# RWKV heads: GpSimd masks behind the spread of blocks, four things in other places, two projection steps moved

## The chip, the cores and the metric

One core of a Trainium2 chip. The metric is the device time of one execution of the whole program, in microseconds. A core has five engines with queues of their own that meet only at semaphores: TensorE (PE, matrix products into eight PSUM banks), VectorE (DVE), ScalarE (ACT), GpSimd (POOL) and SyncE (SP, which here only issues DMAs). PEld is TensorE's loading of weights.

## The reference, cut to what matters

The program is a two-layer trunk: in each layer three token mixers side by side (SSD, RWKV-7, neighbourhood attention), a gated merge, and a mixture of experts. Only the RWKV mixer is touched. It computes, for 16 heads of width 64, in two directions, over 256 context and 256 latent tokens:

```
p = p + mu * bi_shift(p);  r, k, v, wl, al, gl = split(p)
w = -softplus(-(w0 + tanh(wl) @ w2)) - 0.5;  decay = exp(-exp(w))
a = sigmoid(a0 + al @ a2);  g = sigmoid(gl) @ g2
kk = normalise(k * k_k);  k_dir = k * (1 + (a - 1) * k_a)
S = S * w_t - (S kk_t) (kk_t * a_t)' + v_t k_t';  y_t = S r_t      # scan, both directions
yn = (y - mean) * rsqrt(var + eps) * ln_w + ln_b
out = (yn + bonus) * g
```

In layer 0 outputs are wanted for all 512 tokens, in layer 1 for the 256 latent ones only.

## The kernel before, in words

`rwkv_heads` (from line 1679) does a layer in eight turns, one for each pair of heads (128 channels on the 128 partitions). The scan is done in chunks of 64 tokens, eight chunks (`NC`), two heads and two directions at a time. Within a chunk the delta rule needs the inverse of a triangular 64x64 matrix. It is made from 16x16 blocks on VectorE (`block_inverses`, lines 2558 to 2581: transposes, small products, and the spread of the blocks into their place, line 2580 and its neighbours), and widened to 64 with products on TensorE in four stages (`STAGES`; TensorE's `inverse(b, g)`). ScalarE and VectorE take each stage's products out of PSUM (`EVACUATIONS`: "copy" is ScalarE's line 2277, "vcopy" VectorE's line 2590, "eye" adds the unit matrix on VectorE, line 2594). Then the inverse is applied (`apply_inverse`; the result leaves PSUM by ScalarE's line 2287 and VectorE's line 2599), the chunk products are made, and `crossing` carries the state over the chunks in six chain steps (TensorE `step`, VectorE `chain`, line 2619).

The order of the work is written out by hand. Each engine has a function `mix(b, c, ...)` for a turn, in which b is the turn whose scan is carried out and c the next one, whose features are prepared beside it. TensorE's `filler(n)` puts n projection steps of turn c (24 in all: three column groups of eight steps, each a product of 128x128 weights with 512 tokens; in layer 1 the last group has 256 tokens) into places at which it would otherwise wait. In the last turn, which has no c, the filler does 40 steps of gate projections of 512 (layer 1: 256) tokens instead, and the tuple `LAST` says how many at each call. An assertion holds that all steps are done.

The places that the change touches:

- GpSimd's `masks` (line 2419) multiplies the gram matrices by triangular masks, four instructions (line 2417). It waits until VectorE has transposed the first of two results of the block inverse (`X_TURNED`, step 28 of 33 of semaphore `small`, line 2575). VectorE's second transpose (2577) and the four instructions of line 2580 follow.
- ScalarE's `root` (line 2294) turns the variance of a finished turn into a reciprocal root: a logarithm (line 2296, from PSUM bank `SUM_BANK` = 0) and an exponential (line 2298). It stands in the next turn's `mix`, behind `key_grams(b, 1)`. TensorE waits for the logarithm (semaphore `vlog`) before `decay_and_rate(0)` writes the same bank (lines 1846, 1847). The variance product is line 2044.
- ScalarE's `gate` copies the gate product out of bank 4 (line 2193). It stands behind `keep_middle(c, 0)` (line 2180) and the load of the logarithm's table (line 2330). TensorE's `gram_times_v` waits for it and for VectorE's `bound_norm` (line 2473), as both banks are written anew.
- VectorE's `mix` (line 2631): `shift_key` (lines 2453, 2455) stands before `inverse(b, 1)`, and `apply_inverse` (line 2599) behind `shift_mix(3)` (2464), `unit_key` (2487) and two `key` (2491). ScalarE's `key_square` (2189) and the second `decay_and_rate` (2184, 2185) wait for the shifted key, and TensorE's gate product (line 1851) for those.
- VectorE's `out` (lines 2625, 2628, 2629) finishes the turn before, and `bonus` (line 2515) takes bank 3 out, for which the third group of products in stage 1 waits.
- GpSimd's other work in a turn: `inner_decays` (2399, 2400), `receptance` (2406), `copy_receptance` (2413).

Of the kernel before, what the change touches and what calls it, by code (L numbers as in the profile page):

```python
# [1678 lines left out]
def rwkv_heads(k, y, t0):  # L1679
# [9 lines left out]
    with ExitStack() as st:  # L1689
# [129 lines left out]
        def _(pe):  # L1819
# [167 lines left out]
            def crossing(b, c, kept, filler):  # L1987
                if b:
                    hold(s.g3in, b(4, 4))
                    hold(s.rin, b(2, 2))  # L1990
                    step(b, 1)
                    filler(2)
                    step(b, 2)
                if c:
                    hold(s.rawin, kept)
                    value_turns(c)
                if b:
                    filler(1)
                    step(b, 3)
                    for pos in range(1, 4):  # L2000
                        for z in range(2):
                            across(z, pos)
                if c:
                    key_turns(c, 0)
                if b:
                    filler(1)
                    step(b, 4)
                    for z in range(2):
                        across(z, 4)
                if c:  # L2010
                    key_turns(c, 1)
                if b:
                    filler(2)
                    step(b, 5)
                    for z in range(2):
                        across(z, 5)
                if c:
                    left_turns(c)
                if b:
                    step(b, 6)  # L2020
                    for z in range(2):
                        across(z, 6)
                if b and not c:
                    filler(2)
                if c:
                    hold(s.rdec, c(2, 2))
                    gram_pair(c, 0, 0, [(s.tok, c(8, 5)), (s.tok, c(8, 6))])
                if b:
                    for z in range(2):
                        hold((s.st0, s.st1)[z], b(6, 6))  # L2030
                        across(z, 7, s.y_done if z else None)
                if c:
                    gram_pair(c, 0, 1, [(s.tok, c(8, 7)), (s.tok, c(8, 8))], s.gdone)
                    gram_other(c)
                    if b:
                        filler(2)
                        variance(b)
                    for part in range(2):
                        gram_pair(c, 1, part, [] if part else [(s.nevac, c(6, 6)), (s.nevac, c(6, 5))], s.gdone)
                    bonus(c)  # L2040
# [2 lines left out]
                pe.wait_ge(s.sq, b(1, 1))  # L2043
                mm(k.bank[SUM_BANK][:, 0:n], const(k, "headones"), yq[:, t0:], start=True, stop=True).then_inc(s.var_d, 1)

            LAST = (7, 7) + 13 * (2,)

            def mix(b, c, raws, ended, gating=False):
                at = [0, 0]

                def late_gates(count):
                    for _ in range(LAST[at[1]]):
                        i, kt = at[0] // KT, at[0] % KT
                        if kt == 0:
                            hold(tile_in[LATE_PLACE[i]], 16 * LATE_LOADS[i])
                            if i < 2:
                                hold(s.rawin, raws)
                            else:
                                hold(s.sig_done, i - 1)
                            if i == 1:  # L2060
                                hold(s.gevac, b(4, 4))
                        gate_step(3 + i, kt, LATE_PLACE[i], LATE_BANKS[i], s.gate_done)
                        at[0] += 1
                    at[1] += 1

                def filler(count):
                    if not c:
                        late_gates(count)
                        return
                    for _ in range(count):  # L2070
                        j, kt = STEP_ORDER[at[0] // KT], at[0] % KT
                        if kt == 0:
                            hold(w_in[j], b(16, 16))
                        if at[0] == 0:
                            hold(s.rawin, raws)
                        if at[0] == KT:
                            hold(s.gevac, b(4, 4))
                        if at[0] == 2 * KT:
                            hold(s.rawin, b(3, 7))
                        if gating:  # L2080
                            gate_step(at[0] // KT, kt, j, RAW_BANK[j], s.proj)
                        else:
                            projection_step(j, kt)
                        at[0] += 1

                filler(4)
                if c:
                    hold(s.low_in, c(32, 32))
                    if ended:
                        hold(s.vlog, ended(1, 1))  # L2090
                    decay_and_rate(0, RATE_BANKS)
                filler(4)
                inverse(b, 0)
                filler(1)
                inverse(b, 1, filler)
                filler(1)
                if c:
                    hold(s.wa_in, c(4, 2))
                    decay_and_rate(1, RATE_BANKS)
                inverse(b, 2)  # L2100
                if c:
                    gate_and_norm(c)
                filler(1)
                if c:
                    hold(s.gate_in, c(1, 1))
                    hold(s.normin, c(1, 1))
                gram_times_v(b)
                inverse(b, 3)
                filler(1)
                apply_inverse(b)  # L2110
                filler(1)
                chunk_products(b, filler)
                inside(b)
                crossing(b, c, b(3, 8), filler)
                assert at[0] == (3 * KT if c else 5 * KT), at

# [50 lines left out]
        def _(act):  # L2167
# [23 lines left out]
            def gate(c, at):  # L2191
                act.wait_ge(s.gate, c(1, 1))
                ac(y[:, at, t0:], one(k.bank[GATE_BANK][:, 0:n]), ACT.Copy).then_inc(s.gate_in, 1)
# [100 lines left out]
            def root(b):  # L2294
                act.wait_ge(s.var_d, b(1, 1))
                ac(yq[:, t0:], k.bank[SUM_BANK][:, 0:n], ACT.Ln, scale=1.0 / 64, bias=fixed[:, 1:2]).then_inc(s.vlog, 1)
                act.wait_ge(s.vlog, b(1, 1))
                ac(yq[:, t0:], yq[:, t0:], ACT.Exp, scale=-0.5).then_inc(s.root, 1)

# [8 lines left out]
            def mix(b, c, at, ended, gating=False):  # L2308
                key_grams(b, 1)
                if ended:  # L2310
                    root(ended)
                if c:
                    act.wait_ge(s.pcd, c(1, 1))
                    keep_middle(c, 1)
# [8 lines left out]
                if c:  # L2323
                    keep_middle(c, 2)
                    key_square(c)
                    decay_and_rate(1, c, RATE_BANKS)
                    key_rates(c)
                    act.wait_ge(s.vb, b(MIX_STEPS, SET_UP + 1))
                    keep_middle(c, 0)
                    nc.scalar.preload_act_table_set("natural_log")  # L2330
                    gate(c, at)
                    inverse_norm(c)
                gram_times_v(b)
                if not c:
# [15 lines left out]
                if c:  # L2350
                    gram(c)
                    keep(STEP_ORDER[2], c, b(3, 9), gating=gating)
                    key_grams(c, 0)
                    off_blocks()
                else:
                    root(b)

            first = turn_value(0)
            act.wait_ge(s.derived, 1)
# [34 lines left out]
        def _(pool):  # L2394
# [22 lines left out]
                tt(ops[:, h, j, chunks], ops[:, h, j, chunks], spread(mask(name, h), chunks.stop - chunks.start), ALU.mult).then_inc(s.masked, 1)  # L2417

            def masks(b):
                pool.wait_ge(s.small, b(BLOCK_STEPS, X_TURNED))  # L2420
                pool.wait_ge(s.gevac, b(4, 4))
                for j, name in ((IN_KEY, "strict"), (OUT_KEY, "inclusive")):
                    for h in range(2):
                        with_mask(b, h, j, name)
# [18 lines left out]
        def _(v):  # L2443
# [187 lines left out]
            def mix(b, c, m, f, i, before, ahead):  # L2631
# [3 lines left out]
                    out(m, *before)  # L2635
                bonus(m, b)
                m.settle()
                if c:
                    v.wait_ge(s.rpd, b(2, 2))
                    v.wait_ge(s.rawin, c(3, 3))  # L2640
                    v.wait_ge(s.pcd, c(1, 1))
                    shift_key(f, c)
                inverse(b, 1)
                if c:
                    sums(f, c, 0)
                inverse(b, 2)
                if c:
# [4 lines left out]
                if c:  # L2652
                    shift_sum(f, c, 2)
                    shift_mix(f, c, 2, 2, vv)
                    shift_sum(f, c, 0)
                    shift_mix(f, c, 3, 0, r)
                    unit_key(f, c)
                    key(f, c, 0)
                    key(f, c, 1)
                apply_inverse(b)  # L2660
                if c:
                    f.settle()
                    away(f, c, 0)
                chunk_moves(b)
# [1104 lines left out]
```

## Time and profile before

| | us |
|---|---|
| median of 3 runs | 3647.39 (3645.66 to 3649.04) |
| the profiled execution | 3645.4 |
| its span | 3643.6 |
| mean granted TensorE clock | 0.966 of full |
| RWKV heads, first seven turns, layer 0 | 482.4 |
| RWKV heads, first seven turns, layer 1 | 448.4 |
| the eighth turns' start | 1391.7 and 3158.4 |

Times in rows are microseconds from the span's start. A row of a timeline gives start, duration, engine, line, operation, and the tiles or tensors it writes and reads; "x4" is a run of four instructions merged into a row. What stands in square brackets is the idle time of that engine just before, and what ended it. In the rows of busy time by stretch the columns are: the stretch, its length, the busy time of PE, PEld, DVE, ACT and POOL with their numbers of instructions, the granted clock of TensorE as a share of full speed, the DMA share and GB/s.

### The profile page before, as it was taken

How to read it: one execution, taken by the hardware profiler on the slowest of the kernel's cores; microseconds unless marked ns; L12 is line 12 of the kernel's file. 1: busy time of each engine (PE TensorE's matmuls, PEld its weight loads, DVE VectorE, ACT ScalarE, POOL GpSimd, SP SyncE). 2: the span in 40 equal slices, each digit the busy share in tenths (PEclk: the TensorE clock that was granted, in tenths of full speed). 3: DMA queues.
4: the chain of work that ended last, by engine and by line, in shares of the span. 5: the costliest groups of instructions: out<-in, count | busy, mean ns of one | idle time of the engine just before them, and what ended most of it. 6: DMA issues, size and time to landing. Idle time of an engine off the chain costs nothing. (4 is left out here: it accounts for less than half of the span.)

```text
span 3643.6 us, 72098 instructions
## 1 busy us (share of the span) xinstructions
PE 3283.6 (90%) x31390; PEld 1789.5 (49%) x31390; DVE 1686.4 (46%) x3268; ACT 1082.8 (30%) x1940; POOL 453.5 (12%) x411
## 2 busy tenths in 40 slices
PE   6989999998888889999999697998988888899997
PEld 3454444544555555443332345656655555674333
DVE  3584902664777774220000356834257777631111
ACT  2211001603655653121111321103145656420001
POOL 0051200401111110010000002112011111100000
PEclk8999999999999999999999799999999999899998
DMA  5103623252111111369998211834211111269996
GB/s 205 52 19 110 202 71 96 81 169 57 28 28 30 28 34 54 111 253 420 407 386 345 91 47 47 265 111 110 78 43 28 36 28 30 55 239 383 424 424 275
DMA packets 255436, 537.18 MB, mean 147 GB/s; under 512 B 49520, under 2 KB 173696, under 8 KB 222224
## 3 DMA queue, kind: packets, MB, share of 16 engines
q1 hardware_dynamic: 236064, 463.82, 34.8%
q0 software_dynamic: 19056, 68.69, 5.4%
q8 instruction: 254, 4.16, 0.5%
q14 instruction: 62, 0.51, 0.0%
HBM read 514.59 MB, written 17.87 MB: 146 GB/s over the span
## 5 line engine op out<-in xcount | busy, mean ns | idle before, releaser
L1295 PE MATMUL banks<-sb_h,sb_ring 128*128 128x512 f32 (+1 forms) x1344 | 474.8, 512 | 11.3 <-DMA sb_ring<-w_branch 7.7
L1295 PEld LDWEIGHTS banks<-sb_h,sb_ring 128*128 128x128 f32 x1344 | 254.3, 190 | 225.0 <-issue 195.8
L1832 PE MATMUL banks<-sb_h,sb_ring 128*128 128x512 f32 (+1 forms) x672 | 325.6, 604 | 6.3 <-DMA sb_ring<-w_in 4.1
L815 PE MATMUL banks<-sb_h,sb_ring 128*128 128x512 f32 x512 | 232.6, 613 | 19.4 <-SPq L237 19.4
L1823 PE MATMUL banks<-inv 64*64 64x64 f32 x4864 | 141.9, 233 | 62.1 <-DVE inv L2594 37.8
L1823 PEld LDWEIGHTS banks<-inv 64*64 64x64 f32 x4864 | 121.6, 145 | 140.5 <-issue 139.3
L3393 DVE TENSOR_TENSOR hrow<-hrow,banks 128x256 f32<-128x256 f32 x36 | 15.1, 421 | 356.2 <-ACT hrow L3429 356.2
L3241 PE MATMUL banks<-gu,xs 128*64 128x512 f32 x768 | 169.3, 594 | 4.1 <-DMA gu<-gu_pairs 3.6
L1832 PEld LDWEIGHTS banks<-sb_h,sb_ring 128*128 128x128 f32 x672 | 119.4, 197 | 108.5 <-issue 92.4
L1295 PE MATMUL banks<-sb_branch,sb_ring 128*128 128x512 f32 (+1 forms) x512 | 170.9, 487 | 0.0
L815 PEld LDWEIGHTS banks<-sb_h,sb_ring 128*128 128x128 f32 x512 | 100.0, 198 | 139.1 <-issue 118.4
L578 DVE SCALAR_TENSOR_TENSOR sc<-vtok,first_silu,sc 128x1024 f32<-128x1024 f32 x112 | 149.3, 1374 | 7.0 <-DMA vtok<-w_mod 1.2
L3521 PE MATMUL banks<-gu,xs 128*32 128x512 f32 x1368 | 150.1, 592 | 2.2 <-ACT xs L3414 2.2
L1295 PEld LDWEIGHTS banks<-sb_branch,sb_ring 128*128 128x128 f32 x512 | 96.9, 190 | 68.7 <-issue 60.6
L1525 DVE TENSOR_TENSOR sb_acc<-zs,banks 128x512 f32<-128x512 f32 (+1 forms) x16 | 8.9, 553 | 251.8 <-PE banks L1295 251.8
L1295 PE MATMUL banks<-sb_ring,sb_h 128*128 128x512 f32 x256 | 110.2, 592 | 0.0
L3241 PEld LDWEIGHTS banks<-gu,xs 128*64 128x64 f32 x768 | 53.8, 137 | 113.8 <-issue 101.1
L3521 PE MATMUL banks<-sb_ring,xs 128*32 128x512 f32 x936 | 103.8, 593 | 1.4 <-ACT xs L3414 0.8
L1837 PE MATMUL banks<-sb_h,sb_ring 128*128 128x512 f32 (+1 forms) x256 | 103.9, 535 | 0.0
L2417 POOL TENSOR_TENSOR ops<-ops,sb_consts 128x512 f32<-128x512 f32 (+1 forms) x64 | 72.9, 1170 | 247.5 <-DVE inv L2575 247.5
L1115 DVE SCALAR_TENSOR_TENSOR W<-W,sb_cols 128x512 f32<-128x512 f32 x128 | 100.7, 787 | 4.5
L3521 PEld LDWEIGHTS banks<-gu,xs 128*32 128x32 f32 x1368 | 48.9, 110 | 98.6 <-issue 95.7
(502 smaller groups left out, 5641.2 us busy)
## 6 DMA issues: line engine op xcount, KB each, us to landing
gu<-gu_pairs SPq DMA_DIRECT2D x64, 1536.0 KB, 16.8
gu<-gu_tiles SPq DMA_DIRECT2D x57, 1024.0 KB, 9.3
sb_ring<-w_in SPq DMA_DIRECT2D x24, 2048.0 KB, 9.3
sb_ring<-gu_tiles SPq DMA_DIRECT2D x39, 1024.0 KB, 9.9
vtok<-w_mod POOLq DMA_DIRECT2D x64, 512.0 KB, 5.6
sb_ring<-down_pairs SPq DMA_DIRECT2D x32, 1024.0 KB, 14.7
sb_ring<-w_in SPq DMA_DIRECT2D x58, 512.0 KB, 3.9
sb_ring<-down_tiles SPq DMA_DIRECT2D x25, 1024.0 KB, 8.5
```

Source lines behind the costliest of these rows:

```text
L578: do.put(nc.vector.scalar_tensor_tensor(self.acc[c], tile, by, self.acc[c], ALU.mult, ALU.add))
L815: m = mm(k.bank[j], k.ring[:, h, kt, P * j:P * j + P], k.h[:, kt], start=kt == 0, stop=kt == KT - 1)
L1115: tap.do(stt(out, src, w, out, ALU.mult, ALU.add))
L1295: mm = nc.tensor.matmul(out, left(kt), right(kt), start=kt == 0, stop=kt == KT - 1)
L1525: tt(k.acc[:, t, t0:], sg[:, t % 2, t0:], projs[0][t % 2][:, 0:n], ALU.mult).then_inc(s.merged, 1)
L1823: m = mm(k.bank[bank][H[to], at:at + w], left, right, start=start, stop=True, skip_group_check=True)
L1832: m = mm(k.bank[banks[j]][:, WHOLE[j]:], w[:, j, kt], k.h[:, kt, WHOLE[j]:], start=kt == 0, stop=kt == KT - 1)
L1837: m = mm(k.bank[bank][:, t0:], parts.tiles[place][:, kt], k.h[:, kt, t0:], start=kt == 0, stop=kt == KT - 1)
L2417: tt(ops[:, h, j, chunks], ops[:, h, j, chunks], spread(mask(name, h), chunks.stop - chunks.start), ALU.mult).then_inc(s.masked, 1)
L3241: m = mm(wide[i][rows[e], :], xs[:, kt, rows[e]], cols[:, 512 * i:512 * i + 512], start=kt == 0, stop=kt == KT - 1)
L3393: nc.vector.tensor_tensor(h, h, wide[i][:, 256:512], ALU.mult).then_inc(s.mul, 1)
L3521: m = mm(banks[i][32 * j:32 * j + 32], left[:, P * i + 32 * j:P * i + 32 * j + 32], w[:, e], start=start, stop=stop)
```

## The change

```diff
 TensorE, crossing:
                 if b:
-                    filler(1)
                     step(b, 3)
...
                 if b:
-                    filler(1)
                     step(b, 4)
...
-            LAST = (7, 7) + 13 * (2,)
+            LAST = (8, 8) + 9 * (2,) + (3, 3)
...
                     decay_and_rate(0, RATE_BANKS)
-                filler(4)
+                filler(6)
                 inverse(b, 0)

 ScalarE:
             def root(b):
                 act.wait_ge(s.var_d, b(1, 1))
                 ac(yq[:, t0:], k.bank[SUM_BANK][:, 0:n], ACT.Ln, scale=1.0 / 64, bias=fixed[:, 1:2]).then_inc(s.vlog, 1)
+
+            def root_end(b):
                 act.wait_ge(s.vlog, b(1, 1))
                 ac(yq[:, t0:], yq[:, t0:], ACT.Exp, scale=-0.5).then_inc(s.root, 1)
...
                 key_grams(b, 1)
                 if ended:
-                    root(ended)
+                    root_end(ended)
...
                     key_rates(c)
+                    gate(c, at)
+                    nc.scalar.preload_act_table_set("natural_log")
                     act.wait_ge(s.vb, b(MIX_STEPS, SET_UP + 1))
                     keep_middle(c, 0)
-                    nc.scalar.preload_act_table_set("natural_log")
-                    gate(c, at)
                     inverse_norm(c)
...
                     keep(STEP_ORDER[2], c, b(3, 9), gating=gating)
+                    root(b)
                     key_grams(c, 0)
                     off_blocks()
                 else:
                     root(b)
+                    root_end(b)

 GpSimd:
             def masks(b):
-                pool.wait_ge(s.small, b(BLOCK_STEPS, X_TURNED))
+                pool.wait_ge(s.small, b(BLOCK_STEPS, BLOCK_STEPS))
                 pool.wait_ge(s.gevac, b(4, 4))

 VectorE, mix:
                 m.settle()
+                inverse(b, 1)
                 if c:
...
                     shift_key(f, c)
-                inverse(b, 1)
-                if c:
                     sums(f, c, 0)
                 inverse(b, 2)
...
                     shift_sum(f, c, 0)
+                apply_inverse(b)
+                if c:
                     shift_mix(f, c, 3, 0, r)
                     unit_key(f, c)
                     key(f, c, 0)
                     key(f, c, 1)
-                apply_inverse(b)
-                if c:
                     f.settle()
                     away(f, c, 0)
                 chunk_moves(b)
```

The work of each engine is the same as before. The logarithm of a turn's variance now stands in that turn's own crossing, before the gram copies of the next; the exponential stays where it was.

## Rows read from the trace of the kernel before

**Rows 1.** The page, busy time of each engine over the whole span.
```profile
PE 3283.6 (90%) x31390; PEld 1789.5 (49%) x31390; DVE 1686.4 (46%) x3268; ACT 1082.8 (30%) x1940; POOL 453.5 (12%) x411
```
**Rows 2.** Busy time by stretch: seven turns of layer 0, seven of layer 1.
```profile
909.32:1391.68 482.36, 417.28 (x9020) 263.79 (x9019) 355.50 (x710) 280.05 (x448) 81.14 (x71) 0.97 0.12 31
2710.04:3158.43 448.39, 369.78 (x8525) 250.97 (x8523) 338.11 (x711) 265.88 (x448) 73.67 (x70) 0.95 0.13 35
```
**Rows 3.** TensorE's waits, layer 0's seven turns: releaser, total us, times, longest.
```profile
PE banks L1823 <- DVE inv L2594: 21.6, 7, 3.4
PE banks L1950 <- DVE inv L2599: 15.2, 7, 2.2
PE banks L1823 <- ACT sb_branch L2193: 9.7, 7, 1.4
PE banks L1823 <- ACT inv L2261: 8.0, 6, 1.3
```
**Rows 4.** The same view, layer 1's seven turns.
```profile
PE banks L1950 <- DVE inv L2599: 18.1, 7, 2.8
PE banks L1823 <- DVE inv L2594: 15.3, 7, 2.5
PE banks L1823 <- ACT sb_branch L2193: 11.7, 7, 2.0
PE banks L1823 <- ACT inv L2261: 11.3, 6, 1.9
```
**Rows 5.** Timeline of a layer 0 turn: masks, and VectorE's spread before and beside them.
```profile
1046.83 5.06 POOL L2417 TENSOR_TENSOR ops<-ops,sb_consts 128x512 f32<-128x512 f32 x4 [15.09 <-DVE inv L2575]
...
1044.19 1.45 DVE L2573 TENSOR_SCALAR inv<-x,sb_consts 64x256 f32<-64x256 f32 x4
...
1048.56 3.76 DVE L2580 TENSOR_SCALAR inv<-inv,sb_consts 64x256 f32<-64x256 f32 x4
```
**Rows 6.** Timeline at 881 us (GpSimd, VectorE), and line 2497 in a turn.
```profile
881.21 3.08 POOL L2406 TENSOR_TENSOR cc<-cc,rkv 128x512 f32<-128x512 f32 x2 [30.77 <-ACT cc L2214]
...
881.41 1.75 DVE L2497 TENSOR_TENSOR sb_ring<-bb 128x512 f32<-128x512 f32 x1
...
1081.63 0.68 DVE L2497 TENSOR_TENSOR sb_ring<-bb 128x512 f32<-128x512 f32 x1
```
**Rows 7.** Timeline of TensorE behind its wait for line 2594.
```profile
1055.17 1.81 PE L1832 MATMUL banks<-sb_h,sb_ring 128*128 128x512 f32 x2
1056.91 2.96 PE L1823 MATMUL banks<-inv 64*64 64x64 f32 x64
1059.80 1.13 PE L1832 MATMUL banks<-sb_h,sb_ring 128*128 128x512 f32 x2
```
**Rows 8.** Timeline, the shifted key and what follows it on ScalarE.
```profile
1057.51 0.75 DVE L2455 SCALAR_TENSOR_TENSOR rkv<-sb_ring,pc,rkv 128x512 f32<-128x512 f32 x1
...
1058.30 0.72 ACT L2189 ACTIVATE sb_ring<-rkv,pc 128x512 f32<-128x512 f32 x1 [0.46 <-DVE rkv L2455]
...
1062.06 0.69 ACT L2184 ACTIVATE sb_ring<-banks,pc 128x512 f32<-128x512 f32 x1 [3.04 <-PE banks L1847]
```
**Rows 9.** Timeline of ScalarE around the gate copy.
```profile
1066.80 0.60 ACT L2193 ACTIVATE sb_branch<-banks 128x512 f32<-128x512 f32 x1
```
**Rows 10.** Timeline of VectorE and GpSimd around the applied inverse and the chunk moves.
```profile
1073.21 0.75 DVE L2464 SCALAR_TENSOR_TENSOR rkv<-sb_ring,pc,rkv 128x512 f32<-128x512 f32 x1
...
1075.98 1.28 DVE L2599 COPY inv<-banks 128x512 f32<-128x512 f32 x2
...
1077.37 2.85 POOL L2406 TENSOR_TENSOR cc<-cc,rkv 128x512 f32<-128x512 f32 x2 [6.70 <-ACT cc L2214]
...
1078.63 0.69 DVE L2605 TENSOR_TENSOR inv<-banks,sb_consts 128x512 f32<-128x512 f32 x1 [0.77 <-PE banks L1950]
```
**Rows 11.** Timeline of ScalarE, the table loads of the root.
```profile
1040.64 1.28 ACT L2296 ACT_TABLE_LOAD   x1
...
1042.64 1.28 ACT L2298 ACT_TABLE_LOAD   x1
```

## Prediction

> **What bounds the kernel now.** I read the page first: TensorE is busy for 90% of the span, every other engine for under half [rows 1]. That is a mean over stages, and the change touches one stage, the RWKV heads. It runs twice (layer 0 from about 909 us, layer 1 from about 2710 us), each time in eight turns. So the second view is the busy time of the first seven turns of each layer: 482.4 us with 417.3 us of TensorE in layer 0, 448.4 us with 369.8 us in layer 1 [rows 2]. TensorE stands idle for 65.1 us and 78.6 us there, 9.3 us and 11.2 us a turn, in turns of 68.9 us and 64.1 us. Its mean granted clock is 0.97 and 0.95 of full; with the two levels 2.4 and 1.2 GHz that is 2 x 0.03 x 482 = 29 us and 2 x 0.05 x 448 = 45 us at the lower one. VectorE is busy for 50.8 us and 48.3 us of a turn and so not far behind. All that can be won is in these 144 us of waits, in at most half of those 74 us of slow clock, and in little beside it.
>
> Third view: whom TensorE waits for. In layer 0 it is the eye addition of VectorE after the first inverse product (21.6 us), the copies of the applied inverse (15.2), the gate copy of ScalarE (9.7), and the spread of blocks (8.0) [rows 3]. In layer 1 it is 15.3, 18.1, 11.7 and 11.3 us for the same four [rows 4]. That leaves 65.1 - 54.5 = 10.6 us and 78.6 - 56.4 = 22.2 us of short waits, 1.5 us and 3.2 us a turn. The parts of the diff meet these rows one by one, so the question is what is late next in each place.
>
> **GpSimd masks behind the spread of blocks.** Now the four masks start when the first transposed block is there (1046.83 us) and last 5.06 us; in that time VectorE's four spread instructions of 64x256 take 3.76 us, while four of the same size, written from another tile, took 1.45 us just before them, with GpSimd idle [rows 5]. They wait for each other's operands in SBUF. Moved behind, the spread takes 1.45 us: 2.3 us earlier in each turn. But the 5.06 us of masks (4.03 us in layer 1, where two have half the columns) then lie beside what VectorE does next: the eye addition (one operand in PSUM), then the three instructions of the last turn's output, then the bonus. I look for such instructions beside GpSimd work: at 881 us an addition with both operands in SBUF took 1.75 us beside GpSimd's products, and the same line alone 0.68 us [rows 6]. The outputs' three instructions have both operands in SBUF. The chunk moves, additions with an operand in PSUM, took 0.69 us beside the same GpSimd line [rows 10]. So I price the eye addition at nothing, and the output's three instructions at one GpSimd boundary each, between 0 and 3 x 1.07 = 3.2 us; masks of 1.27 us, begun 1.6 us before the first of the three, leave room for about 2.1 us in layer 0 and 1 us in layer 1. The bonus stands behind them on VectorE, and the third product group of inverse stage 1 waits for the bonus (bank 3). So: TensorE's wait for the eye addition (3.1 us a turn) falls to about 0.5 us, and a new wait for the bonus of 2.0 us (layer 0) and 0.8 us (layer 1) comes behind it.
>
> **Two projection steps moved.** filler(4) becomes filler(6) before the first inverse product; the two single steps in the crossing go. A step of 512 columns is about 1.1 us of TensorE alone [rows 7], a little less in a run of steps. The sum of the work is the same, but some 2 us of it now cover the wait for the spread (1.1 to 1.6 us a turn) and the wait for the logarithm below. Steps 9 and 10 wait for the fourth gram copy, done two microseconds and more before they are reached, and for weights that SyncE asked for a turn earlier; no DMA moves against another. In the crossing nothing uncovers: between two chain steps there still lie 64 transposing cells of 1.0 us, and VectorE answers a chain step in about 0.9 us. In layer 1 the steps that leave the crossing have 256 columns, and those in the chunk products get 256 instead of 512, so TensorE comes to the first chain step 0.9 us earlier, and may wait there. In the last turn there are no transposing cells between the steps: two uncovered answers cost about 0.5 us in layer 0, and in layer 1 two more steps fill part of a wait of 4.1 us. I take -1 us for both together.
>
> **Variance logarithm.** It moves from the next turn's start to the crossing, before the gram copies; its exponential stays. ScalarE now does load, logarithm, load, exponential behind the gram copies, and TensorE, whose decay product needs the same bank, waits up to 0.8 us. Now the logarithm is done some 5 us earlier and that wait goes. The gram copies come 0.7 us (layer 0) and 1.2 us (layer 1) later; nobody is waiting there, as the masks are moved too. ScalarE reaches the spread of rows earlier by about 1.3 us, of which VectorE can use 0.7 us, and only in layer 0. Each of the two functions is preceded by a load of 1.28 us of its own now, so pulling them apart adds none [rows 11].
> (The Trainium skill, "ScalarE: Activation LUTs", section "Table sets: the hidden batching unit", says that a logarithm followed by an exponential needs one load, since one set has both. By that rule pulling them apart would add a load a turn, 14 x 1.28 = 18 us of ScalarE. The trace disagrees: both loads stand there already.)
>
> **Gate copy.** Before the second stage's end TensorE waits for the gate copy, which stands behind a middle copy (0.6 us) and a table load (1.28 us as in [rows 11]) and starts at 1066.80 [rows 9]. Moved before both, it is ready 1.9 us earlier. The same wait is also for the bounded norm of VectorE, which is then the later one, about at the end of the filler step: the wait of 1.4 to 1.7 us goes to about 0.
>
> **Inverse stage 1 before the key shift.** The two copies of stage 1 (0.6 us each, as the two of the same size in [rows 10]) now stand before the key shift of 1.5 us. Behind the shift hang ScalarE's square (0.7) and the two second rates (1.3 together), and behind those the gate product [rows 8]. After the last product T of stage 1: second copy T + 0.7, shift T + 2.2, rates T + 4.2; TensorE itself has a step, the rates' product and stage 2, T + 3.2. Its wait there, among the short ones now, becomes about 1.2 us.
>
> **Applied inverse's copies.** They now stand behind four instructions that come to 2.8 us (1073.21 to 1075.98) [rows 10]. In front of them they end 2.3 to 2.8 us earlier, and TensorE's wait of 2.2 to 2.6 us goes to 0.3 or 0.5. But those four are still to be done before the chunk moves, for which VectorE waited only 0.8 us [rows 10]. The chunk moves come earlier by less than TensorE does. And GpSimd's two pairs of SBUF products (inner decays, receptance) now fall on VectorE instructions with both operands in SBUF, since VectorE no longer waits for TensorE in between: about 0.9 us each by the price of [rows 6]. So VectorE gets late with the chunk sums, and the first chain step waits 1.5 us (layer 0) or, with TensorE's 0.9 us and less work in the half-width stage, 3.3 us (layer 1).
>
> **The sum.** Waits of TensorE a turn after, layer 0: 0.5 + 2.0 + 1.2 + 0.3 + 1.5 + 0.4 (what stays of the short ones) = 5.9, before 9.3: -3.4 x 7 = -24 us. Layer 1: 0.5 + 0.8 + 1.2 + 0.5 + 3.3 + 1.9 (what stays of the short ones) = 8.2, before 11.2: -3.0 x 7 = -21 us. Last turns -1 us. Clock: after the eye addition's wait in the turn at 1046.83 a step and 64 cells took from 1055.17 to 1059.80, 4.6 us, where they take 2.1 to 2.2 at full clock [rows 7]; the granted clock was half there. Up to 37 us are paid so over both layers. The longest wait of a turn falls from 3.0 us to 2.0 (layer 0), but a new one of 3.3 us comes in layer 1; I take a bit under half back, -16 us. Together -62 us against the profiled execution's 3645.4 us: 3583.4. That execution is 2 us below the median 3647.39, so 3585 us for the median.
>
> **Rivals.**
> (a) The masks and GpSimd's products disturb nobody: the terms 2.0 and 0.8 go, and 1.5 and 3.3 become 0 and 1.8. That is 7 x 3.5 + 7 x 2.3 = 41 us more: 3544. For it: eye additions and copies from PSUM are undisturbed in every row. Against it: [rows 6].
> (b) VectorE's tail is longer than I have it, 1.5 us a turn, and no clock comes back: 3585 + 21 + 16 = 3622. For it: VectorE would be busy for 49 of 60 us in layer 1, in a row from the applied inverse to the chunk sums.
> (c) All waits are only exchanged, 0 us: 3647. For it only that TensorE's work is unchanged and 9 of each 10 us; against it that about 1.1 us of the spread's wait and 1.4 us of the gate's go without any successor on their engine.
> (d) Slower: the clock. My new waits lie at four places of a turn instead of two or three, each followed by small products. A stretch at half clock has cost 2.5 us [rows 7]. There are now about 74 / 3.4 = 22 of them. Without any clock gain the time is 3601; it takes 18 more, 1.3 a turn, to reach 3647. At two more a turn it is 3601 + 28 x 2.5 = 3671. Against it: the idle share of TensorE falls in all of this.
> That the logarithm is not earlier at all, because ScalarE gets to it before the sum is made, would need the variance product later than the third projection; it is directly behind it, 1.0 us, less than the load of 1.28 us.
>
> **Chances.** Forecast 0.52, (a) 0.18, (b) 0.16, (c) 0.07, (d) 0.07. A difference of under 0.2% (7 us) can't be told from none here. Faster by more: 0.52 + 0.18 + 0.16 and a little of (c) = 0.87; same 0.06; slower 0.07. Range: from (a), 3542, to just over (b), 3625.
>
> **What would show it.** The spread instructions of line 2580 at 0.36 us each; the output's three instructions above 1 us each in layer 0; TensorE waiting for the bonus and for the chunk sums, not any more for the gate copy, and little for the eye addition and the applied copies; turns of about 64 us and 60 us. Wrong if the output's instructions stay at 0.7 us (then (a)), if the first chain step waits more than 4 us, or if the mean clock of the turns falls.

## The result

| kernel | median us | runs | ratio to before, 95% interval |
|---|---|---|---|
| before | 3647.85 | 4 | |
| changed | 3594.72 (3590.16 to 3597.80) | 4 | 0.9854 (0.9837 to 0.9871) |

The change makes the kernel 53 us faster; forecast were 62. The profiled execution's span goes from 3643.6 to 3588.4 us. In the two profiled executions, from start to start of TensorE's first product in each stage:

| stage | before | changed | us won |
|---|---|---|---|
| up to the heads of layer 0 (same program) | 0 to 834.62 | 0 to 832.22 | 2.4 |
| heads of layer 0 | 834.62 to 1440.25 | 832.22 to 1412.87 | 25.0 |
| from there to the heads of layer 1 (same program) | to 2640.13 | to 2610.61 | 2.1 |
| heads of layer 1 | 2640.13 to 3196.28 | 2610.61 to 3141.21 | 25.6 |
| to the end (same program) | to 3643.6 | to 3588.4 | 0.1 |

So 50.6 of the 55.2 us between these two executions are won in the heads. The other 4.6 us lie where nothing was changed: the profiled execution of the changed kernel is the fastest of its four.

Line numbers move with the edit. The masks are line 2419 now (2417 before), the spread 2582 (2580), the eye addition 2596 (2594), the output 2627, 2630 and 2631 (2625, 2628, 2629), the bonus 2517 (2515), the applied copies 2601 (2599), chunk moves 2607 and 2608 (2605, 2606), chunk sums 2613 (2611), second rates 2183 (2185), spread of blocks on ScalarE 2259 (2261), bounded norm 2475 (2473), gate copy 2191 (2193), logarithm 2294 (2296).

The changed kernel, busy time by stretch, seven turns of each layer, against [rows 2]:

```profile
909.60:1366.26 456.66, 407.34 (x9020) 258.66 (x9019) 367.72 (x710) 278.99 (x448) 89.02 (x71) 0.99 0.13 34
2680.90:3107.05 426.15, 355.22 (x8557) 247.95 (x8560) 345.95 (x710) 265.00 (x448) 77.64 (x71) 0.97 0.14 38
```

A turn takes 65.2 us instead of 68.9, and 60.9 instead of 64.1. The stretches run from first mask to eighth turn's first mask as before, so in the changed kernel both ends lie some 2.5 us later in their turn. TensorE's idle time falls from 65.1 to 49.3 us and from 78.6 to 70.9 us, and its busy time, with the same work, from 417.3 to 407.3 and from 369.8 to 355.2 us: these 24.5 us go with its clock, whose mean rises from 0.97 to 0.99 and from 0.95 to 0.97.

Whom TensorE waits for in layer 0, to be read beside [rows 3]:

```profile
PE banks L1823 <- DVE bv L2517: 11.5, 6, 2.0
PE banks L1823 <- issue: 10.6, 16, 1.4
PE banks L1823 <- DVE inv L2613: 9.8, 7, 1.7
PE banks L1823 <- DVE inv L2596: 5.1, 7, 0.7
PE banks L1851 <- ACT bb L2183: 5.0, 7, 0.9
PE banks L1823 <- DVE sb_ring L2475: 2.8, 7, 0.5
```

Gate copy, spread of blocks and applied copies are gone; bonus, chunk sums and the bounded norm have come, the second rates have grown, as well as waits on "issue", which the profile can put down to nobody. The same view in layer 1, beside [rows 4]; the longest wait for the spread there, 4.6 us, is the eighth turn's, which lay outside the stretch before:

```profile
PE banks L1823 <- issue: 18.9, 17, 2.5
PE banks L1823 <- DVE inv L2613: 12.3, 7, 2.3
PE banks L1823 <- ACT inv L2259: 9.6, 7, 4.6
PE banks L1851 <- ACT bb L2183: 6.6, 7, 1.3
...
PE banks L1950 <- DVE inv L2601: 3.2, 6, 0.6
```

VectorE beside the masks in a layer 0 turn (the first row is the masks), against [rows 5, 6]:

```profile
1103.48 5.86 POOL L2419 TENSOR_TENSOR ops<-ops,sb_consts 128x512 f32<-128x512 f32 x4 [16.88 <-DVE inv L2582]
...
1102.14 1.26 DVE L2582 TENSOR_SCALAR inv<-inv,sb_consts 64x256 f32<-64x256 f32 x4
1103.70 1.29 DVE L2596 TENSOR_TENSOR inv<-banks,sb_consts 128x512 f32<-128x512 f32 x2 [0.30 <-PE banks L1823]
1104.91 1.63 DVE L2627 TENSOR_TENSOR yb<-yb,rkv 128x512 f32<-128x512 f32 x1
1106.57 1.65 DVE L2630 SCALAR_TENSOR_TENSOR yb<-yb,ln,bv 128x512 f32<-128x512 f32 x1
1108.25 1.64 DVE L2631 TENSOR_TENSOR sb_branch<-yb,sb_branch 128x512 f32<-128x512 f32 x1
1109.93 0.69 DVE L2517 SCALAR_TENSOR_TENSOR bv<-banks,rkv 128x512 f32<-128x512 f32 x1
```

The spread takes 1.26 us instead of 3.76. The eye additions, with one operand in PSUM, are untouched. The three output instructions, with both operands in SBUF, take 1.64 us each instead of 0.7. The four masks start at 1103.48, 1104.71, 1105.94 and 1107.63, and the last ends at 1109.34; each output instruction ends some 0.6 us after the end of one of them, as it would if it waited for one mask to end.

### The profile page after: what moved, and what is told of

Same layout as the page of the kernel before. It is cut to its first block and busy times, and to the rows that moved or that the text cites. A ratio compares the mean times of both kernels' runs of the same rounds, so it can differ in the third digit from the quotient of the medians.

```text
span 3588.4 us, 72098 instructions
## 1 busy us (share of the span) xinstructions
PE 3255.4 (91%) x31390; PEld 1776.3 (50%) x31390; DVE 1703.0 (47%) x3268; ACT 1080.6 (30%) x1940; POOL 465.4 (13%) x411
## 5 line engine op out<-in xcount | busy, mean ns | idle before, releaser
L1295 PE MATMUL banks<-sb_h,sb_ring 128*128 128x512 f32 (+1 forms) x1344 | 474.9, 512 | 11.2 <-DMA sb_ring<-w_branch 7.6
L1832 PE MATMUL banks<-sb_h,sb_ring 128*128 128x512 f32 (+1 forms) x672 | 310.4, 586 | 8.8 <-DMA sb_ring<-w_in 4.0
L1837 PE MATMUL banks<-sb_h,sb_ring 128*128 128x512 f32 (+1 forms) x256 | 97.6, 514 | 2.0 <-ACT bb L2306 2.0
## 6 DMA issues: line engine op xcount, KB each, us to landing
gu<-gu_pairs SPq DMA_DIRECT2D x64, 1536.0 KB, 16.6
```

The costliest lines, as they stand in the source:

```text
L1295: mm = nc.tensor.matmul(out, left(kt), right(kt), start=kt == 0, stop=kt == KT - 1)
L1832: m = mm(k.bank[banks[j]][:, WHOLE[j]:], w[:, j, kt], k.h[:, kt, WHOLE[j]:], start=kt == 0, stop=kt == KT - 1)
L1837: m = mm(k.bank[bank][:, t0:], parts.tiles[place][:, kt], k.h[:, kt, t0:], start=kt == 0, stop=kt == KT - 1)
```

## The experiments

All ratios are to the kernel before, timed beside each; the changed kernel's is 0.9854. "Slower" and "faster" without more are against the changed kernel. Most kernels here are the changed kernel with one part as it was. Line numbers in rows are those of each kernel's own text. The stretches of a kernel run from its first mask to its eighth turn's first mask. Outside the heads, where all kernels are the same, two profiled executions can differ by 7 us (e3 against the changed kernel, between the layers), so a few us of a single profile prove nothing.

**The two steps back (e1).**

```diff
+                    filler(1)
                     step(b, 3)
...
+                    filler(1)
                     step(b, 4)
...
-                filler(6)
+                filler(4)
```

> The changed kernel (3595 us) with the two projection steps back in the crossing. In the changed kernel TensorE has short waits for nothing recorded ('issue') of 10.6 us (layer 0) and 21.3 us (layer 1) in the seven turns, before the change 2.7 and 10. Theory I: they come from the supply of instructions. In the crossing TensorE now runs hundreds of small products in a row, and the two long steps that used to let the supply catch up are gone. Then with the steps back the issue waits fall to about 3 and 10 us, the wait for the spread of blocks returns with 1 to 1.6 us a turn, and the time is 3600 to 3608. Theory II: the issue waits have come because TensorE waits less in general, wherever the steps stand. Then they stay at 10 and 20 us, the 1.9 us a turn of moved work are lost in full, 14 x 1.9 = 27 us, and the time is about 3620.

Measured: 3611.4 us, 0.9900 (0.9884 to 0.9917): 17 us slower than the changed kernel, between the theories. TensorE's waits on "issue" in it, layer 0 and then layer 1:

```profile
PE banks L1823 <- issue: 3.5, 9, 0.9
...
PE banks L1885 <- issue: 1.0, 1, 1.0
PE banks L1832 <- issue: 0.5, 1, 0.5
...
PE banks L1823 <- ACT inv L2261: 19.8, 7, 5.5
...
PE banks L1823 <- issue: 11.9, 14, 2.0
```

In all they are 5.0 us (12.2 in the changed kernel, 2.7 before) and 13.5 us (22.6, 10.2). So most of the new issue waits (16 of 22 us) come from the place of the steps, as theory I has it. They don't stand in the crossing alone: the changed kernel has 10.9 us of them at the small products of line 1823 that read `ops` (the chunk products above all), where 2.6 us stood before. The wait for the spread of blocks is back with 9.0 and 19.8 us. In the changed kernel 0 and 9.6 us of it are left: the moved steps win 19 us of waits there and pay 16 us of issue waits. Nearly all of what the stretches lose (14 us) is TensorE's busy time, 410.5 and 365.2 us in e1, 13 us more than in the changed kernel for the same work; its clock is 0.95 instead of 0.97 in layer 1, and 0.99 in both in layer 0.

**The masks back (e2), and the masks alone (e11).** The wait of `masks` is `b(BLOCK_STEPS, X_TURNED)` again; in e11 the kernel before gets only the new wait.

> The changed kernel with GpSimd's masks again behind the first transposed block. Theory I (the masks only change their victim): line 2582 takes 3.7 us for four instead of 1.3, the output's three instructions 0.7 us each instead of 1.64, the wait for the bonus (2.0 us a turn in layer 0) goes and the one for the eye addition becomes about 3 us (2.4 in layer 1). In waits that is +0.3 us a turn in layer 0 and +1.8 in layer 1, 15 us together, and with it some of the half clock stretches come back, up to 15 us: 3610 to 3625. Rival: the two places cost the same, 3595 within 5.

Measured: 3632.2 us, 0.9958 (0.9944 to 0.9973), 37 us slower than the changed kernel and more than either theory. The four spread instructions take 4.19 us, the output's 0.68, 0.75 and 0.69, as expected. By stretch:

```profile
909.59:1375.15 465.56, 409.77 (x9020) 261.00 (x9019) 370.90 (x711) 278.50 (x448) 84.81 (x70) 0.98 0.13 32
2693.05:3143.94 450.89, 373.86 (x8529) 259.13 (x8527) 349.13 (x711) 264.39 (x448) 76.70 (x71) 0.93 0.14 35
```

Layer 0 loses 8.9 us. Layer 1 loses 24.7 us, and 18.6 of those are TensorE's busy time, with its clock down from 0.97 to 0.93. The wait for the eye addition is back in every turn, 2.0 us on average. In some turns the granted clock falls behind it (0.64 from 2763.17 to 2766.50 us; the step takes 2.07 us, where the same step took 1.12 just before):

```profile
2761.65 1.59 PE L1823 MATMUL banks<-inv 64*64 64x64 f32 x64 [2.32 <-DVE inv L2596]
2763.17 2.07 PE L1832 MATMUL banks<-sb_h,sb_ring 128*128 128x512 f32 x2
2765.17 2.26 PE L1823 MATMUL banks<-inv 64*64 64x64 f32 x64
```

It is not a rule: in layer 0 the same wait is longer, 3.0 us a turn, and the busy time there rises by 2.4 us only.

> The kernel before with only the masks moved behind the spread of blocks. Undoing this part in the changed kernel cost 37 us, the four undoings together 80 us where the whole change brought 53. Theory I (the parts lie on one chain, each is worth most when the others are in): alone the masks bring 3 us less of waiting for the eye addition a turn, but the first inverse product still waits for the spread, and the output delayed by 2.8 us takes most back in layer 0: 3625 to 3637. Rival (the masks' part acts by itself, mainly on the clock): 3605 to 3615.

Measured: 3620.7 us, 0.9932 (0.9911 to 0.9952), 24 us faster than before and a little outside theory I. By stretch:

```profile
910.56:1393.45 482.89, 421.91 (x8970) 264.28 (x8962) 356.78 (x710) 280.53 (x448) 85.78 (x70) 0.96 0.13 32
2711.75:3140.29 428.54, 358.46 (x8523) 247.84 (x8515) 334.56 (x710) 267.08 (x448) 74.93 (x70) 0.97 0.14 35
```

In layer 0 the part is worth nothing (482.9 us against 482.4 in [rows 2]): the stall is only exchanged, 11.0 us of waiting for the bonus come for 16.6 us less for the eye addition, and the clock is worse. All of it comes in layer 1, 448.4 to 428.5 us, where half-width instructions keep the bonus off the path.

**VectorE's orders back: both (e3), and the key shift alone (e7).**

> The changed kernel with both of VectorE's orders as before (key shift ahead of inverse stage 1, applied inverse's copies behind the four feature instructions). Theory I (VectorE's tail is the bound, so the earlier copies win little): TensorE's wait for the copies returns with 2.2 to 2.6 us a turn, but its wait for the chunk sums (9.8 and 12.3 us over the turns) and part of that for the second rates (5.0 and 6.6) go: 3600 to 3608. Rival: the wait for the copies was the price, 14 x 2.4 = 33 us: 3625 to 3630.

Measured: 3606.1 us, 0.9891 (0.9874 to 0.9907), 11 us slower. As theory I has it the wait for the applied copies is back and the one for the chunk sums gone. Layer 0, then layer 1:

```profile
PE banks L1950 <- DVE inv L2601: 18.6, 7, 2.9
...
PE banks L1950 <- DVE inv L2601: 21.5, 7, 3.4
```

> The changed kernel with the key shift again ahead of inverse stage 1, and the applied inverse's copies left where the change put them. Theory I (the two reorderings of VectorE have opposite signs, the shift's is a loss): TensorE's wait for the second rates falls from 5.0 and 6.6 us to 2 and 2, stage 1's copies come 1.4 us later and inverse stage 2 with them in part: 3588 to 3596. Rival: the shift's move won as much as it should, and undoing it costs the 11 us that undoing both together cost: 3603 to 3608.

Measured: 3595.5 us, 0.9860 (0.9844 to 0.9877), no difference. The wait for the second rates falls to 1.9 and 2.0 us, by 7.7 us together, and the time stays. So the key shift's move is worth nothing either way, and what e3 loses belongs to the applied copies, if the two parts add. How much that is stays less sure than the 11 us: in the profiled executions the heads of both layers together take 4.7 us more in e3 than in the changed kernel, of 14 us between the two executions, and the rest lies where the program is the same. The applied copies' move removed 37 us of waits; 22 were handed on to the chunk sums.

**ScalarE's places back (e4).**

> The changed kernel with logarithm and gate copy in their old places on ScalarE. Theory I: the gate copy's wait of 1.4 to 1.7 us a turn returns (21 us) less the wait for the bounded norm that stands in its place now (6 us), and the logarithm's (up to 0.8 us a turn, and 0.7 us of the spread of rows in layer 0), 8 us: 3613 to 3620. Rival: ScalarE's delays are taken up by VectorE's, which is late anyway in the same turn: 3595 to 3600.

Measured: 3611.4 us, 0.9903 (0.9886 to 0.9919), 17 us slower. The gate copy's wait is back with 9.8 and 11.7 us and the logarithm's with 4.7 and 2.0; the chunk sums' falls by 5 us. Theory I's mechanism, with a time 2 us below its range.

**No masks (e8), and two other places for them (e5, e6).**

> The changed kernel without the masks' four instructions (the gram matrices stay unmasked, so this part of the computation is left out); GpSimd only reports them done. It is the floor of what any place for the masks can give. Theory I: the output's instructions 0.7 us each, no wait for the bonus, everything behind unchanged: 2.0 us a turn in layer 0 and 0.5 to 0.8 in layer 1, 3570 to 3580. Rival (my case (a) of free masks, with a clock gain): 3550 to 3560.

Measured: 3582.3 us, 0.9829 (0.9812 to 0.9847): 12 us is all that the masks' new place still costs, and the two intervals overlap. The mechanism is theory I's, the time 2 us above its range. All of it is in layer 0, whose heads are 13 us shorter in the profiled execution; layer 1's are not. In layer 0 no bonus wait is left, and the chunk sums are waited for about as in the changed kernel (9.4 us, there 9.8).

> The changed kernel with the masks one place later still: GpSimd waits for VectorE's bonus, behind the output's three instructions. Theory I (each pair of SBUF operands of VectorE beside the masks costs a GpSimd boundary, wherever it stands): the output's instructions fall from 1.64 to 0.7 us and TensorE's wait for the bonus (11.5 us in layer 0) goes, but the key shift's two instructions, now beside the masks, grow from 0.7 to about 1.6 us each, and the wait for the second rates from 0.3 to 0.9 up by about 1 us a turn: 3585 to 3593. Rival: only the output was exposed, and 2.8 us a turn come back: 3565 to 3575.

Measured: 3603.4 us, 0.9883 (0.9866 to 0.9899), slower than both theories. VectorE's output and key shift:

```profile
1112.44 0.68 DVE L2627 TENSOR_TENSOR yb<-yb,rkv 128x512 f32<-128x512 f32 x1
...
1117.97 1.75 DVE L2455 TENSOR_TENSOR sb_ring<-sb_ring 128x512 f32<-128x512 f32 x1
1119.75 1.64 DVE L2457 SCALAR_TENSOR_TENSOR rkv<-sb_ring,pc,rkv 128x512 f32<-128x512 f32 x1
```

And TensorE's wait for the second rates, layer 0:

```profile
PE banks L1851 <- ACT bb L2183: 18.0, 7, 3.0
```

The mechanism is theory I's. The price was larger, as the shift carries the second rates: TensorE waits 18.0 us for them in layer 0 instead of 5.0. That takes all of the bonus wait's 11.5 us back. The loss itself is in the clock: over the first six turns of layer 0 TensorE's idle time is 0.8 us less than in the changed kernel and its busy time 4.1 us more, for the same work, with a mean clock of 0.97 instead of 0.99.

> The changed kernel in which VectorE does the bonus ahead of the output of the turn before, and that output's three instructions behind the first scan, when the masks are over; the bonus has two buffers for this, and the bounded norm stands ahead of the second scan. Then VectorE works only with PSUM operands while the masks run. Theory I: the output at 0.7 us each, no wait for the bonus, stage 1's copies 3 to 5 us earlier than now in layer 0 and 2 in layer 1; what is won is what TensorE had waited there (2.0 us a turn in layer 0, about 0.5 in layer 1) and a part of VectorE's tail: 3570 to 3582. Rival (VectorE's tail from the applied inverse on sets the turn, whatever comes before): its wait for the chunk sums grows by as much, 3590 to 3597.

Measured: 3613.8 us, 0.9918 (0.9896 to 0.9940), slower than even the rival. The output's instructions are 0.7 us each and nobody waits for the bonus. But they now stand on VectorE's way to the applied inverse, and the tail that follows meets GpSimd's inner decays (first row) and its receptance products, which run from 1130.23 for 3.08 us (second row):

```profile
1125.13 1.65 DVE L2467 SCALAR_TENSOR_TENSOR rkv<-sb_ring,pc,rkv 128x512 f32<-128x512 f32 x1
...
1130.41 3.45 DVE L2494 TENSOR_TENSOR bb<-bb,rkv 128x512 f32<-128x512 f32 x2
```

The two key products take 3.45 us instead of 1.28. TensorE waits 11.7 + 10.3 us (layer 0) and 15.5 + 12.5 us (layer 1) for chunk sums and receptance sums. The loss is layer 1's: its stretch takes 441.4 us instead of 426.2, layer 0's 455.4 instead of 456.7.

**Receptance later (e9).** This is what e6 pointed to.

```diff
-            def receptance(c):
+            def receptance(c, b=None):
                 pool.wait_ge(s.shifted, c(3, 3))
+                if b:
+                    pool.wait_ge(s.g3in, b(4, 4))
```

> The changed kernel in which GpSimd's receptance products wait until VectorE has written the chunk sums. In the changed kernel they stand beside VectorE's first key product with two SBUF operands (1.64 us instead of 0.68), which delays chunk moves and chunk sums, for which TensorE waits 1.4 and 1.8 us a turn. Theory I: that instruction falls to 0.68 us, the wait for the chunk sums and the one for the receptance sums fall by about 1 us a turn together, and the decayed products beside which they now stand have slack in the crossing: 3580 to 3588. Rival: the decayed products stand between the chain steps on VectorE, grow to 1.6 us and hold the chain up by as much: 3592 to 3600.

Measured: 3580.1 us, 0.9816 (0.9798 to 0.9834): faster than the changed kernel by some 14 us. The rows it rests on in the changed kernel, and VectorE's tail in e9:

```profile
1130.02 3.38 POOL L2408 TENSOR_TENSOR cc<-cc,rkv 128x512 f32<-128x512 f32 x2 [5.70 <-ACT cc L2212]
...
1130.61 1.64 DVE L2496 SCALAR_TENSOR_TENSOR bb<-sb_ring,bb 128x512 f32<-128x512 f32 x1
...
1129.69 0.69 DVE L2498 SCALAR_TENSOR_TENSOR bb<-sb_ring,bb 128x512 f32<-128x512 f32 x1
...
1136.38 1.06 DVE L2507 TENSOR_TENSOR bb<-bb,sb_ring 128x512 f32<-128x512 f32 x1
```

The expectation's first key product (`away` in the program) takes 0.69 instead of 1.64 us, a decayed product in the crossing 1.06 instead of 0.68, where nobody waits for it. The wait for the chunk sums falls from 9.8 to 2.6 us and from 12.3 to 5.8. Theory I.

**One step back (e10).** filler(5) in front, filler(1) ahead of chain step 4.

> The changed kernel with one of the two projection steps back in the crossing, ahead of chain step 4, behind which most of the waits on nothing recorded stand; filler(5) ahead of the first inverse product. Theory I (supply of instructions): the issue waits fall from 12 and 23 us to about 8 and 17, the spread of blocks is waited for by 0.3 to 0.9 us a turn more, the sum about even: 3592 to 3600. Rival: half of what both steps back cost, 3602 to 3605, if the front place is worth its full step.

Measured: 3599.0 us, 0.9870 (0.9853 to 0.9888). Issue waits 6.5 and 11.4 us, half of the changed kernel's; the spread's wait 4.4 and 14.4. An even exchange within what can be measured, as theory I has it.

**Receptance later, and the last two masks behind the key shift (e12).**

```diff
                 for j, name in ((IN_KEY, "strict"), (OUT_KEY, "inclusive")):
+                    if c and j == OUT_KEY:
+                        pool.wait_ge(s.kfd, c(1, 1))
```

> The changed kernel with GpSimd's receptance products behind the chunk sums (which alone gave 3580 us), and the last two of the four masks behind the key shift. Theory I (an operand pair beside GpSimd costs one boundary, so it matters only what VectorE does in that place): two of the output's three instructions fall from 1.64 to 0.7 us, TensorE's wait for the bonus in layer 0 from 2.0 to about 0.2 us a turn, and the last masks cost the first scan about 1 us, behind which VectorE was idle for 1.4 us in layer 0 but not in layer 1: 3568 to 3576. Rival: what comes earlier is only waited for in VectorE's tail, 3578 to 3583.

Measured: 3577.1 us, 0.9813 (0.9799 to 0.9826), 1 us above theory I's range and 1 below the rival's. That is the lowest median here, but not told apart from e9. The wait for the bonus is 0.4 us in layer 0, and its seven turns take 440.5 us instead of 448.5 in e9. In layer 1 they take 424.3 instead of 420.3:

```profile
1102.48 1.61 DVE L2631 TENSOR_TENSOR yb<-yb,rkv 128x512 f32<-128x512 f32 x1
1104.13 0.75 DVE L2634 SCALAR_TENSOR_TENSOR yb<-yb,ln,bv 128x512 f32<-128x512 f32 x1
1104.91 0.69 DVE L2635 TENSOR_TENSOR sb_branch<-yb,sb_branch 128x512 f32<-128x512 f32 x1
...
1109.89 2.29 DVE L2475 TENSOR_TENSOR_SCAN cc<-sb_consts,sb_ring 128x512 f32<-128x512 f32 x1
```

One output instruction is still held, two are free, and the scan takes 2.29 instead of 1.23 us, behind which VectorE had 1.4 us to spare in layer 0 and nothing in layer 1.

## Why the prediction was right, and where it was off

The time lies in the range, the sign and most of the mechanisms hold. That it came as near as 53 of 62 us is in part luck, as errors of both signs met (see the sum). By its own terms:

- **Masks.** Spread 1.26 us (said 1.45), output held at one boundary each, eye addition untouched, wait for it 0.7 us a turn (0.5): right. The bonus wait is 1.9 us a turn in layer 0 (2.0). In layer 1 I had 0.8 us and no such wait is there. That layer 0 gains nothing by this part alone is shown by e11. (The Trainium skill, "SBUF — State Buffer", section "Who interferes with whom", says that a VectorE instruction with two SBUF inputs contends with a GpSimd instruction that reads SBUF, and one with at most one such input, outside the two-port modes, does not. The trace agrees: 1.63 to 1.65 us for the output's instructions instead of 0.7, and 1.29 us for the two eye additions beside the masks, as before.)
- **Steps.** "The sum of the work is the same" and "in the crossing nothing uncovers" is the step that failed. No semaphore is late there, but TensorE waits on "issue" 12.2 and 22.6 us instead of 2.7 and 10.2: 22 us more, which no term had. e1 and e10 show that 16 of them go with the steps. Nor is the wait for the spread of blocks covered in full: 9.6 us of it stay in layer 1, 4.6 of those in the eighth turn. One of the issue waits, in a layer 0 turn of the changed kernel:

```profile
1143.19 0.63 PE L1823 MATMUL banks<-sb_consts,bb 64*64 64x64 f32 x25
1144.84 0.80 PE L1823 MATMUL banks<-sb_consts,bb 64*64 64x64 f32 x37 [1.02 <-issue]
```

  TensorE stops for 1.02 us within a run of like products, between whose members the program has no wait. That fits a supply of instructions which falls behind in long runs of small products and catches up behind long ones; that it is the supply was not measured by itself and stays argued. The trace doesn't confirm it: from 1143.8 to 1144.9 us it has no DMA packet at all, and the nearest two of the instruction queue lie before and behind the stop.
- **Logarithm, gate copy.** Both waits are gone, and the bounded norm is next: 2.8 and 3.2 us, where I had about 0. Undoing both costs 17 us (e4). One load of 1.28 us stands before each of the two functions in the changed kernel too, so pulling them apart added none. (The Trainium skill, "ScalarE: Activation LUTs", section "Table sets: the hidden batching unit", has one load for both; the trace of neither kernel agrees.)
- **Key shift.** The wait for the second rates is 5.0 and 6.6 us, 0.7 to 0.9 a turn (said 1.2). The part is worth nothing (e7).
- **Applied copies.** The wait went to 0 and 3.2 us (said 2 and 3.5). VectorE's tail took over as said: chunk sums and receptance sums 11.0 us in layer 0 (10.5) and 15.3 in layer 1 (23). The price of GpSimd beside it (0.9 us twice) was met: 1.36 and 1.64 us for instructions of 0.68, so 0.7 and 1.0.
- **Sum.** Over the fourteen turns idle time went down by 16 and 8 us instead of 24 and 21, mainly for the issue waits, which a shorter tail in layer 1, the bonus there and the second rates paid back in part. The clock gave 24.5 us instead of 16. That makes 48 us instead of 61. The profiled executions differ by 55, not 48: 4.6 us are won where the program is the same, which is not the change's doing, and the rest in the heads outside the stretches, for which I had 1. The clock's term was a guess between two bounds, and it erred to the other side than the waits.
- **Rivals.** Free masks (a): excluded by the output's 1.64 us, and e8 bounds what free masks would have brought at 12 us. The longer tail (b): it was shorter, and clock came back. All waits exchanged (c): the idle time fell by 24 us in all. The clock (d): it went the other way; its price of 2.5 us a stretch can't be a mean either, as 22 such stretches would make 55 us, where the same text has at most 37 us at stake.

## What to carry to other kernels

Ask of a VectorE instruction beside GpSimd work where its operands lie. In these traces one with two in SBUF was held for up to one GpSimd instruction (0.4 to 1.1 us more each), the four of the spread, from SBUF to SBUF with a scalar, took 2.5 us more together, and one with an operand in PSUM took no longer. Then place GpSimd's work beside PSUM readers, or where VectorE has time to spare. Parts on one chain are not additive: here the four undoings cost 17, 37, 11 and 17 us, 82 in all, where the whole is worth 53, and the masks' part is worth 37 us undone but 24 alone (e11). When fillers are moved out of a run of small products, count the run's instructions too, as it may be waiting for those rather than for a semaphore.

## What the runs showed that I had not expected

- A wait of 2 us in each turn can cost more than itself: with the masks back, TensorE's idle time in layer 1 rises by 6.1 us and its busy time, for the same work, by 18.6 us. In layer 0 it rises by 6.5 us and the busy time by 2.4 only; why the two layers differ stays open.
- A scan is held like other pairs of SBUF operands: 2.29 instead of 1.23 us, in e12.
- Waits on "issue", mostly within runs of 64x64 products, about 20 of them in seven turns of a layer, of 0.6 us on average in layer 0 and 1.0 in layer 1. One long step put back in the crossing halves them (e10, 6.5 and 11.4 us). Two leave 5.0 and 13.5 us (e1): in layer 1, where these steps have 256 columns, the second brings nothing.
- The clock decides experiments whose waits come out even: e1 and e5 lose mainly in TensorE's busy time.
